# Expert weights at the end of the mixer: the wait for the stored rows moves ahead of the second matrix

## What is computed

```python
h = h + m_lat[2] * y                                  # y: the mixer's output
v = modulate(rmsnorm(h, norm_ffn[l]), m_lat[3], m_lat[4]).reshape(B * S, D)
f = hier_moe(v, rt_w_grp[l], rt_b_grp[l], rt_w_exp[l], rt_b_exp[l], ex_w1[l], ex_w3[l], ex_w2[l])
h = h + m_lat[5] * f.reshape(B, S, D)
# inside hier_moe, for every block of tokens that chose expert e:
#   (silu(xb @ w1[e]) * (xb @ w3[e])) @ w2[e]
```

## Time and profile before

| | us |
|---|---|
| median of 3 runs | 2502.25 |
| lowest, highest | 2495.03, 2509.82 |
| the profiled execution, its own time | 2497.47 |
| its span, first to last instruction | 2495.5 |

### The profile page before, as it was taken

How to read it: one execution, slowest core, us unless ns; L and a number is a source line. 1 busy time by engine, 2 the same in 40 slices (tenths; PEclk the granted TensorE clock), 3 DMA queues, 4 the chain that set the end, 5 groups by cost and what they waited for, 6 DMA issues and landing times. The chain is left out here.

```text
span 2495.5 us, 32789 instructions
## 1 busy us (share of the span) xinstructions
PE 2318.0 (93%) x13953; PEld 1017.0 (41%) x13954; DVE 1093.4 (44%) x2267; ACT 361.1 (14%) x645; POOL 298.1 (12%) x317
## 2 busy tenths in 40 slices
PE   5999999989999999999999899999999999999992
PEld 3555455454555523333333444444555323323331
DVE  1788377767845422222222353434454222222225
ACT  2210333331012200000000230000121000000002
POOL 2000000001000222122220000000002212222100
PEclk8999999999999999999999899999999999999996
DMA  9577111020130599999999521113107999999976
GB/s 314 193 258 268 34 26 26 17 110 34 68 152 34 214 353 401 397 412 413 393 411 404 193 90 51 47 37 109 51 34 282 385 403 400 402 401 405 408 321 252
DMA packets 139949, 574.22 MB, mean 230 GB/s; under 512 B 16898, under 2 KB 41782, under 8 KB 88216
## 3 DMA queue, kind: packets, MB, share of 16 engines
q1 hardware_dynamic: 119496, 526.48, 54.7%
q0 software_dynamic: 20224, 45.34, 4.9%
q10 hardware_dynamic: 80, 0.26, 0.0%
HBM read 550.74 MB, written 38.03 MB: 236 GB/s over the span
## 5 line engine op out<-in xcount | busy, mean ns | idle before, releaser
L1677 PE MATMUL ps<-arena 128*32 128x512 f32 x6144 | 683.6, 601 | 29.4 <-DMA arena<-in_ex_w_dram 29.4
L1677 PEld LDWEIGHTS ps<-arena 128*32 128x32 f32 x6144 | 201.4, 111 | 476.4 <-issue 476.4
L1701 PE MATMUL ps<-arena 128*32 128x512 f32 x3072 | 338.9, 592 | 4.0 <-DMA arena<-in_ex_w_dram 3.9
L2418 DVE TENSOR_TENSOR arena<-arena,ps 128x512 f32<-128x512 f32 x48 | 52.5, 1093 | 517.0 <-PE ps L1677 517.0
L1812 PE MATMUL ps<-arena 128*128 128x512 f32 x616 | 264.5, 592 | 0.0
L1557 PE MATMUL ps<-arena 128*128 128x512 f32 x512 | 229.4, 598 | 1.6 <-DVE arena L2212 1.6
L1701 PEld LDWEIGHTS ps<-arena 128*32 128x32 f32 x3072 | 106.8, 110 | 227.2 <-issue 227.2
L795 POOL DMA_INDIRECT arena<-normed_rows,arena x184 | 185.8, 1010 | 79.4 <-issue 55.1
L2463 DVE TENSOR_TENSOR arena<-ps,gates 128x512 f32<-128x512 f32 x96 | 61.8, 686 | 293.7 <-PE ps L1701 293.7
L1812 PEld LDWEIGHTS ps<-arena 128*128 128x128 f32 x616 | 117.0, 190 | 147.3 <-issue 147.3
L1370 PE MATMUL ps<-arena 128*128 128x512 f32 x384 | 167.3, 593 | 0.7 <-issue 0.7
(11 more groups left out here) (314 smaller groups left out, 2156.7 us busy)
## 6 DMA issues: line engine op xcount, KB each, us to landing
arena<-in_ex_w_dram SPq DMA_DIRECT2D x384, 1024.0 KB, 10.5
arena<-in_mod_w_dram SPq DMA_DIRECT2D x24, 2048.0 KB, 8.9
arena<-expert_rows SPq DMA_DIRECT2D x16, 1024.0 KB, 8.6
arena<-in_od_w_in_dram SPq DMA_DIRECT2D x12, 1024.0 KB, 5.3
arena<-in_x_dram SPq DMA_DIRECT2D x2, 4096.0 KB, 14.7
normed_rows<-arena POOLq DMA_DIRECT2D x16, 512.0 KB, 2.9
arena<-in_ev_w_in_dram SPq DMA_DIRECT2D x3, 2048.0 KB, 13.6
arena<-in_ev_w_in_dram SPq DMA_DIRECT2D x12, 512.0 KB, 4.1
```

The costliest lines, as they stand in the source:

```text
L1677: ins = nc.tensor.matmul(bank(2 + m)[c:c + n], x[:, j, c:c + n], w_slot(e % 2, m, KC, FE)[:, j], start=j == 0, stop=j == KC - 1)
L1701: ins = nc.tensor.matmul(bank(5 + half)[c:c + n], HT[:, j * P + c:j * P + c + n], w_slot(e % 2, 2, FC, D)[:, j, half * 512:(half + 1) * 51 ...
L2418: return V.tensor_tensor(HS.rearrange("t (c p) -> t p c", p=P), SL.rearrange("t (p c) -> t p c", c=FC), bank(3).rearrange("t (p c) -> t p ...
```

## The change

In both layers the two waits for the stored rows stand ahead of the second of the three matrices in place of behind the third. So of the six DMAs that follow the last residual, two are issued at once (w1 of expert 0), and four (w1 of expert 1; then w3 of expert 0 in the first layer, w2 of expert 0 in the second) only when all eight tiles of scaled rows have landed in `normed_rows`. No DMA is added, removed or put in another order within its queue.

```diff
@@ -553,11 +553,11 @@
                 weights(1, 2)
                 sp.wait_ge(h_ready, 2 * TT * (l + 1))
                 weights(0, 0)
+                sp.wait_ge(hn_out[0], 16 * (TT // 2) * (l + 1))
+                sp.wait_ge(hn_out[1], 16 * (TT // 2) * (l + 1))
                 weights(1, 0)
                 weights(0, 2 if l else 1)
                 sp.wait_ge(lg_mm, TT * (l + 1))
-                sp.wait_ge(hn_out[0], 16 * (TT // 2) * (l + 1))
-                sp.wait_ge(hn_out[1], 16 * (TT // 2) * (l + 1))
                 sp.wait_ge(x_full[0], gathered(l, 0))
                 weights(1, 1)
```

## The result

The changed kernel takes 2513.01 us in the median of 20 runs (2508.49 to 2521.93), the kernel before 2504.22 in the median of 20 (2495.03 to 2517.03). The ratio is 1.0034, 95% interval 1.0021 to 1.0047: 8.5 us slower, 5.3 to 11.8. Forecast were 5.5 us. The measured 0.34% lies within the 0.5% that the prediction takes for "the same", but with 20 runs of each kernel the loss is clear of no change. Timed again later (6 runs), the ratio came out at 1.0049.

A forecast was written before the change was run, and what follows sets the result against it. TensorE and the DMA engines bound the expert stages almost equally, so the start of L1711 was priced: 1.6 + 2.5 us later plus 1.4 of clock, 2502.25 + 5.5 = 2507.8 us, range 2496 to 2516.

The forecast's parts named there:

- The bound and the mechanism: Expert stages: TensorE and DMA almost equally bound; delaying TensorE's first product moves the whole stage; queueing moves from store to gather.
- The store: Last store of rows in each layer: lands after 2.9 to 4.1 us instead of 8.6 and 8.4.
- The gather's start: First gather on GpSimd, limited by VectorE's table of rows: starts 0.49 and 0.18 us earlier.
- The gather's way: First gather beside the held weights: lands later, so L1711 begins 1.6 and 2.5 us later in the two layers.
- The even share of bytes: Gather sharing evenly with the weight queue: lands 0.8 us sooner in each layer, sum 3.9 instead of 5.5 us.
- The upper bound: Gather takes the slow store's full 9.1 us: L1711 moves by 2.3 and 3.2 us, with the clock 6.9.
- The clock: Second layer: longer idling, 4.6 us, lowers TensorE's clock, so L1711 takes 3.39 instead of 1.96 us; 1.4 us added.
- The size: Whole kernel: 1.6 + 2.5 + 1.4 = 5.5 us slower, 2507.8 us on the median.
- the gather slips through: Rival at the first gather: it keeps its earlier pace; 2.1 us faster, 2500.2 us; chance 0.27.
- the hold does not free the store: Rival: two leading DMAs alone keep the store at about 8 us; 7.5 us slower, 2509.8; chance 0.10.
- TensorE's clock stays down: Rival in spare products and L1677 of pass 0: up to 38 us slower, 2540; chance 0.05.

The follow-up runs named there:

- Experiment 1: Changed kernel with the held matrices also waiting for the first gather, so nothing of SyncE stands in front of it; 1.0076 of the kernel before.
- experiment 6: Changed kernel with the hold one matrix later: four DMAs issued at once, two held until the rows are stored; 1.0038 of the kernel before.
- experiment 7: Changed kernel with the hold one matrix earlier: all six DMAs wait until the rows are stored; 1.0045 of the kernel before.
- experiment 8: Against the changed kernel: five of the six DMAs issued at once, the sixth held behind the first gather; 0.9995 of the kernel before.
- experiment 5: The changed kernel timed and traced again without any edit; 1.0049 of the kernel before.
- experiment 10: The change in the second layer alone, the first layer's waits staying behind the third matrix; 1.0005 of the kernel before.
- experiment 11: Against experiment 8: in the second layer w3 of expert 1 goes ahead of the held half of w2 of expert 0; 0.9982 of the kernel before.

## Why the prediction came out as it did

**The bound and the mechanism were right.** Both openings were slower, and what follows was shifted; the expert stages took 1.2 and 2.3 us more, within their scatter. The loss went from the store, where the work on the table covered it, to the gather. Experiment 1 shows it by its absence (4.2 to 4.5 us with an empty queue against 8.2 to 9.4), experiment 6 by a hold that does nothing for the store and costs the same, the table in experiment 7 by three groups of openings that do not overlap.

**The store** landed after 3.2 to 4.2 us (2.9 to 4.1 forecast), the held DMAs were asked for at +3.3 and +4.3 (3.5). **The gather's start** gained 0.08 us in the second layer (0.18 forecast). In the first it was 0.7 us later: the granted clock fell to 0.50 (1.2 GHz) within 2 us of the store's issue in this execution, and the table was ready at +9.23 in place of +8.21. Whether the change has a part in that is open: it shows in 6 of the 26 openings traced, 4 of 12 with a hold ahead of the store and 2 of 14 without (both in experiment 8), and in none of the six that keep the order of the kernel before. In experiment 5 the gather's start is at +9.23 and +9.17, 0.33 and 0.08 earlier where 0.49 and 0.18 were forecast; it follows the table by 1.0 us and not by 0.86.

**The gather's way** was forecast at 8.5 us to L1711 in both layers; it is 8.2 and 8.6 in one execution, 9.4 and 9.1 in the other. The even share of bytes that the prediction weighs, 0.8 us shorter, would give 7.7, and no opening with held weights is under 8.2. DMA: Bandwidth & Descriptors (Trainium skill, section Queues, rings and completion order) says that a DMA engine changes queue packet by packet, and this the traces bear out: the even share is one of packets. Beside the store of the kernel before (window 844:846), then beside the gather of the changed kernel (window 1904:1906), the two queues move nearly equal numbers of packets, and q1 moves two to three times the bytes because its packets are larger (8.0 KB against 4.1, 7.7 against 2.7):

```profile
q1 hardware_dynamic: 70, 0.56, 68.2%
q0 software_dynamic: 68, 0.28, 33.8%
...
q1 hardware_dynamic: 82, 0.63, 74.5%
q0 software_dynamic: 84, 0.23, 28.7%
```

The upper bound, 9.1 from the phases of the slow store, was the better value for the execution of experiment 5; the first one is as forecast. I had let the held stream drain in front of the gather; its queue also carries the four gathers of pass 1, issued right behind, which move bytes in the same microseconds. By +17 of the first layer of experiment 5 q0 had moved 0.61 MB, more than the gather's 0.52, and L1711 began only at +18.7. That the gathers of pass 1 took the difference is likely by this, but no run takes them away.

**The clock** fell in both layers as forecast. L1711 took 3.64 in place of the forecast 3.39 (3.64 and 3.48 in experiment 5).

**The size.** 5.5 were forecast, 8.5 timed, 7.8 in traces of like kind. By the traces of the first kind the terms are: L1711 later by 2.7 and 3.1 (1.6 and 2.5 forecast, together 1.7 short), the clock and spares 0.4 and 1.5 (0 and 1.4, together 0.5 short). So the mis-sized term is the gather's way under a full queue (1.4 of the 1.7; the other 0.3 is its start), which I took below its upper bound; with the bound, the sum of 6.9 would have come nearer. The two medians (2507.8 forecast, 2513.0) differ by 5.2: 2.0 are the level of the kernel before (2504.22 in place of 2502.25), the rest is this.

**The rivals.** That the gather slips through is refuted by all seven traces with weights held until the rows are stored. That the hold does not free the store did not occur, but experiment 6 built it, at the same cost. That TensorE's clock stays down occurred for the spare products only, in five openings (3.4 to 3.5 us in place of 2.4): both of the first profile, both of experiment 10, one of them without the hold, and one of experiment 7. It never reached the products of pass 0 while the weights for them were there.

## What to carry to other kernels

A wait that clears the way for one transfer puts the held bytes in front of the next. Before moving it, follow the path one step further: ask which transfer ends last for TensorE, what will be on the queues when that one is issued, and whether the stall being cured was covered. The store's 5.7 us of delay cost 0.1 to 0.3 us (by experiment 5), since the table of rows was ready just then; the 3 us that were added to the gather's way cost their full length and the clock besides. What shortened the gather's way to 4.1 to 4.5 us was to give way in front of it with one megabyte; holding back more cost as much in weights that came late. Whether the small gain of experiment 11 would hold when repeated is open.

## What the runs showed of the hardware

- A 512 KB transfer issued by GpSimd while weights stream from SyncE's queue takes 8.3 to 8.9 us to land as a store against 2.9 when the engines are idle. As a gather (to the waiting product) it takes 8.2 to 9.4 us, against 5.4 to 7.6 when the stream ends 3 to 3.5 us after the issue and 4.1 to 4.5 without a stream. Its first bytes come 4 to 4.5 us after its issue beside a stream and 1.5 us without; then the two queues move nearly equal numbers of packets (68 and 70, 84 and 82 in 2 us). Whether 2, 4 or 6 MB had been held made no difference clear of scatter, since in all three cases 2.0 MB or more were moved beside the gather.
- The same program ran in two kinds of execution, with weight loads busy for about 1016 or 1066 us. In the second, the products of pass 0 take 2 to 2.8 us longer, at full granted clock (six of eight openings), or the turning of the rows has gaps of 0.6 to 0.7 us put down to "issue", and the kernel before took 7 us more where such executions were found. The cause is open; that it lies in the chip and not in the program is only likely. Comparing one trace of each gave 13.1 us where the change is worth 8.
- TensorE's granted clock fell to 0.50 for some 3 us right after the last store in 6 of 26 openings, while it was busy without a gap of over 0.3 us, and the table of rows came 1.0 us late. What decides it was not found.
